# The entries of the convolution and of both attentions: order of the first two weight chunks, and of the turn of the second rows

## The reference, cut to what matters

```
u = rmsnorm(h, gain)                 # 256 x 1024
convolution:              a, gate = split(u @ w_in + b_in)      # w_in 1024 x 2048
differential attention:   q, k, v = split(h_normed @ w_qkv)     # w_qkv 1024 x 3072
dilated attention:        q = h_normed @ w_q                    # w_q 1024 x 3072
```

## Time and profile before

| what | value |
|---|---|
| three timed runs, median | 2168.71 us (2168.44 to 2171.89) |
| span of the profiled execution | 2168.2 us (no time of its own beside the span is recorded for it) |
| PE busy | 2138.8 us, 99% |
| DVE / ACT / POOL busy | 1417.4 / 1159.3 / 118.1 us |
| DMA | 371.40 MB, 171 GB/s over the span |

### The profile page before, as it was taken

One profiled execution on the slowest core, in us unless ns is written; L12 is line 12 of the kernel. 1 busy time (PEld: TensorE's weight loads), 2 busy tenths in 40 slices (PEclk: granted clock), 3 DMA queues, 4 the chain that ended last, 5 costly groups with the idle time before them and its releaser, 6 DMA issues.

```text
span 2168.2 us, 28699 instructions
## 1 busy us (share of the span) xinstructions
PE 2138.8 (99%) x11347; PEld 1789.6 (83%) x11347; DVE 1417.4 (65%) x2061; ACT 1159.3 (53%) x1711; POOL 118.1 (5%) x152
## 2 busy tenths in 40 slices
PE   9999999999999999999999999998999999999999
PEld 9878888768888878889877888787888888888887
DVE  7645765576556767657745766686656699675665
ACT  5555544536445645455555544566544565575443
POOL 0000100002000011000000200002100100000000
PEclk9999999999999999999999999999999999999999
DMA  8544655525665436555544655551655566513653
GB/s 267 184 139 163 227 189 190 180 97 181 195 194 170 152 117 195 188 190 183 185 140 159 185 189 190 183 176 59 210 190 187 181 166 188 182 61 117 200 190 115
DMA packets 190068, 371.40 MB, mean 171 GB/s; under 512 B 6993, under 2 KB 126178, under 8 KB 189808
## 3 DMA queue, kind: packets, MB, share of 16 engines
q1 hardware_dynamic: 185776, 358.70, 50.5%
q0 software_dynamic: 4160, 10.86, 2.7%
HBM read 368.48 MB, written 1.05 MB: 170 GB/s over the span
## 4 chain that ended last, share of the span: by engine, by line
PE 91%; DVE 4%; ACT 2%; POOL 1%; issue 1%; DMA 0%; SPq 0%; DVEq 0%; ACTq 0%
PE PS L663 51%; PE PS L795 14%; PE PS L797 7%; PE PS L783 5%; PE PS L833 2%; PE PS L913 1%; DVE wlo L2040 1%; PE PS L840 1%; PE PS L1115 1%; POOL wlo L2904 1%; ACT whi L1484 1%; PE PS L1393 1%; PE PS L1402 1%; PE PS L900 1%; PE PS L1216 1%
## 5 line engine op out<-in xcount | busy, mean ns | idle before, releaser
L2040 DVE TENSOR_TENSOR wlo<-raw,whi 128x1024 fp32r<-128x1024 f32 x658 | 788.7, 1225 | 195.3 <-ACT whi L1484 194.5
L1484 ACT ACTIVATE whi<-raw 128x1024 fp32r<-128x1024 f32 x680 | 700.7, 1055 | 372.3 <-PE PS L663 325.3
L663 PE MATMUL PS<-whi,U 128*128 128x512 f32 x1856 | 523.0, 397 | 7.2 <-DVE U L2078 1.9
L663 PEld LDWEIGHTS PS<-whi,U 128*128 128x128 f32 x1856 | 346.0, 189 | 90.0 <-issue 16.2
L795 PE MATMUL PS<-U,whi 128*128 128x512 f32 x1344 | 334.4, 391 | 0.0
L663 PE MATMUL PS<-wlo,U 128*128 128x512 f32 x928 | 288.2, 392 | 0.0
L795 PEld LDWEIGHTS PS<-U,whi 128*128 128x128 f32 x1344 | 246.6, 188 | 47.5
L2165 DVE TENSOR_TENSOR AR<-PS,AR 128x512 f32<-128x512 f32 x96 | 66.3, 691 | 303.5 <-ACT AR L1571 303.5
L663 PE MATMUL PS<-whi,fH 128*128 128x512 f32 x824 | 256.7, 393 | 0.9 <-DVE fL L2303 0.9
L663 PE MATMUL PS<-wlo,fH 128*128 128x512 f32 x824 | 254.4, 390 | 0.0
L663 PE MATMUL PS<-whi,fL 128*128 128x512 f32 x824 | 254.2, 390 | 0.0
(11 more groups left out here) (333 smaller groups left out, 1959.4 us busy)
## 6 DMA issues: line engine op xcount, KB each, us to landing
raw<-in_mlp_w_up SPq DMA_DIRECT2D x64, 1024.0 KB, 5.4
raw<-in_mlp_w_down SPq DMA_DIRECT2D x64, 1024.0 KB, 4.9
raw<-in_ret_w_in SPq DMA_DIRECT2D x48, 1024.0 KB, 5.2
raw<-in_m_w_up SPq DMA_DIRECT2D x32, 1024.0 KB, 5.4
raw<-in_m_w_down SPq DMA_DIRECT2D x32, 1024.0 KB, 4.9
raw<-in_kv_w SPq DMA_DIRECT2D x24, 1024.0 KB, 5.1
raw<-in_ret_w_out SPq DMA_DIRECT2D x16, 1024.0 KB, 4.7
raw<-in_gla_w_in SPq DMA_DIRECT2D x12, 1024.0 KB, 5.1
```

The lines of the kernel that those rows point to most:

```text
L663: mm = e.matmul(bank(b + nb), a, w[:, nb * 512:(nb + 1) * 512], start=(begins and n < 2), stop=(ends and n >= 4))
L1484: e.activation(split_half(whi, i, x), raw_halves(i)[x], ACT.Copy).then_inc(HI.tick((i, x)), 1)
L2040: e.tensor_tensor(split_half(wlo, i, x), raw_halves(i)[x], split_half(whi, i, x).bitcast(F32), ALU.subtract).then_inc(LO.tick((i, x)), 1)
```

## The change

All of it is in PE's program; ACT, DVE, POOL and SP keep their instructions and their order. The new `gemm_a_two` takes the first two chunks of the three stages together. Its `upper(f, k2, tt)` is the four matmuls of chunk f, half k2, rows tt with `whi` and waits for `HI` and `UL` alone; its `lower(f, k2)` is the four matmuls with `wlo` for both row groups, and signals `USED`. `turn_in` gets a list of pairs, and rows 1 are turned in two portions: pairs 0 and 1 behind the third `upper`, pairs 2 and 3 behind the fifth. The remaining two chunks go through `gemm_a` as before, with `begins=False, k_first=4`, and the convolution's filter products stay behind the third chunk. `PS` has as many matmuls and transposes written to it as before.

```diff
--- before.py
+++ after.py
@@ -746,13 +746,13 @@
...
-            def turn_in(S, tt):
+            def turn_in(S, tt, js=range(4)):
 
                 if tt == 0:
 
                     for ev in turn_free[S]:
                         e.wait_ge(*ev)
-                for j in range(4):
+                for j in js:
                     if S == RET0:
                         e.wait_ge(*s_x[tt][1])
                     else:
@@ -853,6 +853,44 @@
                 turn_in(S, 1)
                 upper(1, 1, 0)
                 upper(0, 0, 1)
+                upper(0, 1, 1)
+                lower(0, 0)
+                lower(0, 1)
+                upper(1, 0, 1)
+                upper(1, 1, 1)
+                lower(1, 0)
+                lower(1, 1)
+
+            def gemm_a_two(S):
+
+
+                i0 = first[S]
+
+                def upper(f, k2, tt):
+                    e.wait_ge(*HI[i0 + f, k2])
+                    k = 2 * f + k2
+                    e.wait_ge(*UL[(S, "in"), tt, k // 2])
+                    w = split_half(whi, i0 + f, k2)
+                    for n, a in enumerate(u_ap(k, tt)):
+                        for nb in range(2):
+                            e.matmul(bank(2 * tt + nb), a, w[:, nb * 512:(nb + 1) * 512], start=(k == 0 and n == 0), stop=False)
+
+                def lower(f, k2):
+                    e.wait_ge(*lo_cut(i0 + f, k2))
+                    w = split_half(wlo, i0 + f, k2)
+                    for tt in range(2):
+                        a_h, _ = u_ap(2 * f + k2, tt)
+                        for nb in range(2):
+                            mm = e.matmul(bank(2 * tt + nb), a_h, w[:, nb * 512:(nb + 1) * 512], start=False, stop=False)
+                    mm.then_inc(USED.tick((i0 + f, k2)), 1)
+
+                upper(0, 0, 0)
+                upper(0, 1, 0)
+                upper(1, 0, 0)
+                turn_in(S, 1, (0, 1))
+                upper(1, 1, 0)
+                upper(0, 0, 1)
+                turn_in(S, 1, (2, 3))
                 upper(0, 1, 1)
                 lower(0, 0)
                 lower(0, 1)
@@ -972,7 +1010,7 @@
                 p, c0 = PC, first[S]
 
                 def filters(c):
-                    if c != 2:
+                    if c != 0:
                         return
                     e.wait_ge(*s_conv_par[CONV_LOADS])
                     e.wait_ge(*UL[(S, "in"), 1, 3])
@@ -1028,7 +1066,8 @@
                     if tt:
                         mm.then_inc(USED.tick((i, k % 2)), 1)
 
-                gemm_a((S, 0), c0, 8, u_ap, (0, 2), fresh=fresh_u((S, "in")), entry=lambda: turn_in(S, 1), after=filters)
+                gemm_a_two(S)
+                gemm_a((S, 0), c0 + 2, 4, u_ap, (0, 2), fresh=fresh_u((S, "in")), begins=False, k_first=4, after=filters)
 
                 def beside(c):
                     if c == 1:
@@ -1219,7 +1258,8 @@
             def pe_diff(S):
                 p, c0 = PD, first[S]
                 k0, k1 = (S, 0), (S, 1)
-                gemm_a((S, 0), c0, 8, u_ap, (0, 2), fresh=fresh_u((S, "in")), entry=lambda: turn_in(S, 1))
+                gemm_a_two(S)
+                gemm_a((S, 0), c0 + 2, 4, u_ap, (0, 2), fresh=fresh_u((S, "in")), begins=False, k_first=4)
                 gemm_a((S, 1), c0 + 4, 8, u_ap, (0, 2), free=([HCP[k0 + (0,)]], [HCP[k0 + (1,)]]), entry=lambda: None)
 
                 def v_product(c):
@@ -1419,11 +1459,12 @@
                                           start=(n == 0), stop=(n == 3), skip_group_check=True)
                     mm.then_inc(VALUE.tick((S, i)), 1)
 
-                for n in range(9):
+                gemm_a_two(S)
+                gemm_a((S, 0), c0 + 2, 4, u_ap, (0, 2), fresh=fresh_u((S, "in")), begins=False, k_first=4)
+                for n in range(1, 9):
                     t = (S, "in") if n < 3 else (S, "kv")
-                    gemm_a((S, n), c0 + 4 * n, 8, u_ap, (0, 2), fresh=fresh_u(t) if n in (0, 3) else None,
-                           free=read_out(n - 1) if n else ((), ()), after=lambda c: beside(n, c),
-                           entry=(lambda: None) if n else (lambda: turn_in(S, 1)))
+                    gemm_a((S, n), c0 + 4 * n, 8, u_ap, (0, 2), fresh=fresh_u(t) if n == 3 else None,
+                           free=read_out(n - 1), after=lambda c: beside(n, c), entry=lambda: None)
 
                 for i in range(16):
                     turn(i)
```

## The result

The changed kernel takes 2172.4 us (median of 20 runs, 2169.14 to 2174.66), the kernel before 2169.47 us beside it (20 runs, 2168.27 to 2171.89): ratio 1.0014, 95% interval 1.0007 to 1.0020. The forecast was 2170.3 us and a difference of +1.6.

A forecast was written before the change was run, and what follows sets the result against it. PE's own stream was taken as the bound, busy 2138.8 of 2168.2 us. Terms +1.8 (differential attention), 0.0 (convolution) and -0.2 (dilated attention) gave +1.6 on 2168.7, so 2170.3 us, range 2167.2 to 2173.2.

The forecast's parts named there:

- Nothing is won ahead of the turn: Differential attention's entry: 0.9 us waiting for ACT replaces 0.24 + 0.68 for POOL; the turn starts at 1390.99 as before.
- Second portion 1.8 us late for ACT and DVE: Behind the turn's second portion, the last lower `U` and everything queued after it on DVE and ACT shift by about 1.8 us.
- Third chunk of the differential attention: PE would start it at 1403.08 after a new wait of 2.4 us, making the stage 1.8 us later.
- PE's own gain: At each entry, four more matmuls and four fewer transposes done by the wait for `U`: some 0.45 us gained.
- Convolution and dilated attention: Slack ahead of the third chunk hides the shift of 1.80 and 1.75 us there; results 0.0 and -0.2 us.
- The three terms: Stage effects: differential attention +1.8, convolution 0.0, dilated attention -0.2 us, summed to +1.6.
- The delay is not given back: Later waits of the differential attention shift along, so 1.8 us stands; rival, given back later: 2168.5 us, chance 0.13.
- the third chunk is bound by DVE: Differential attention: ACT and DVE cannot make up the 1.8 us; rival, not bound by DVE: 2167.2 us, chance 0.13.
- The clock in the new gap, taken as 0: Ahead of the differential attention's third chunk, 2.4 us without matmuls could cost 0 to 3.4 us; 0 taken, little confidence.
- clock falls, short: Rival: PE's clock falls once in the new gap, the shorter fall, costing 1.7 us, so 2172.0 us; chance 0.26.

The follow-up runs named there:

- diff_only: The change kept in the differential attention alone, the other two stages as in the kernel before; 2172.2 us, ratio 1.0011 to the kernel before.
- diff_back: The changed kernel with the old entry back in the differential attention alone; 2168.9 us, ratio 0.9999 to the kernel before.
- again: The changed kernel run once more as it is; 2173.6 us, ratio 1.0016 to the kernel before.
- third_first: The changed kernel, but in the differential attention ACT and DVE make the third chunk's halves ahead of exponentials and head tables; 2168.5 us, ratio 0.9994 to the kernel before.
- turn_earlier: The changed kernel with the second portion of the turn one upper sooner, behind the fourth; 2169.8 us, ratio 1.0000 to the kernel before.
- one_turn: The changed kernel with all four pairs of rows 1 turned at once behind the third upper; 2168.1 us, ratio 0.9990 to the kernel before.
- gap_transposes: The changed kernel with 19 transposes of a constant ahead of the differential attention's third chunk; 2170.9 us, ratio 1.0005 to the kernel before.

## Why the prediction was right, and which term was off

- *Nothing is won ahead of the turn*: right. The turn of rows 1 starts 0.81 us after DVE's first half of `h` in both. ACT's wait in place of POOL's is 0.78 (forecast 0.9).
- *Second portion 1.8 us late for ACT and DVE*: right, 1.80 at every step down the chain.
- *Third chunk of the differential attention*: +1.80 at its start and +1.82 in the stage's length (forecast +1.8). PE follows DVE's start by 1.28 us before and after, where I had carried 1.39; as the same distance stands on both sides, the shift was right all the same, and only the new wait came out at 2.1 us in place of 2.4. diff_only and diff_back put the loss in this stage.
- *PE's own gain*: forecast 0.45, though 4 x 0.227 less half of 1.03 is 0.39. Read from the start of the turn of rows 1, the 48 matmuls of the first two chunks would end 9.73 us later by PE's own pace (1396.28 + 8 x 0.227 - 1388.37), before 10.15: 0.42.
- *Convolution and dilated attention*: 0.0 and -0.2 forecast, 0.0 (-0.06 against again, -0.01 in diff_back against diff_only) and -0.13 measured. The three terms come to +1.7; forecast +1.6.
- *The delay is not given back*, and *the third chunk is bound by DVE*: the stage keeps the whole of it, and third_first frees the chunk by reordering ACT and DVE alone. Both rivals out.
- *The clock in the new gap, taken as 0*: this is the term that was mis-sized. It is 1.5 us in three profiles out of four. The rival "clock falls, short" had 0.26 and the forecast 0.42; the median lies at 2172.4, nearer to that rival (2172.0), and the range held it because it had been drawn to take that rival in. I called idleness of 2.4 us nearer to the wait of 1.4 than to the four one-row matmuls. For those I had also passed over the row just ahead, in the kernel before:

```profile
476.88 1.47 PE L1014 MATMUL PS<-ident,xn 128*128 128x128 f32 x8 [1.06 <-DVE xn L2409]
```

That fall too came behind a stretch in which PE stood idle, 1.06 us of it, and then did eight transposes and the four one-row matmuls; which of these it answers to is open. The Trainium skill, "TensorE: Matmul & The Clock Gate", section "Why this matters for your kernels", warns of idle gaps between bursts of matmuls, but only of gaps longer than this one. By that rule the clock would have stayed up here; in three profiles of four it fell, and the measurement decides. The changed kernel against the one before: +1.7 of delay, and +1.5 in most executions, beside a measured +2.9.
- The forecast stood on a median of three runs, 2168.7; over 20 runs the kernel before is at 2169.5. That is 0.8 us of the distance to 2172.4.

What stays open: how often the clock falls with and without the wait. It also falls in the convolution, for 3.4, 6.8 or 10.2 us: every profile shows one of the three, and the changed kernel's three profiles show all of them. The medians carry that spread; four profiles are no frequency.

## What to carry to other kernels

Before a producer's step is split to give its engine something to do in between, follow the second part down the queues that consume it: everything behind it there moves by the distance between the parts, less the time the consumer needs for the first. Here PE gained 0.4 us and two other queues did everything behind the second part 1.8 us later, which only the stage without slack showed. And a new idle stretch on TensorE may cost more than its length; fill it, or better, give the engine work that waits for nothing new, as the lower parts of rows 0 did here.

## What the runs showed of the hardware

An idle stretch of 2.1 us between dense matmuls was followed by a fall of TensorE's clock from 2.4 to 1.2 GHz in three profiles of four, 0.2 to 1.2 us after PE took up work again, and the stage was 1.5 us longer; waits of 1.1 us and less at the same place (turn_earlier, one_turn) showed none in one profile each, nor did the wait of 1.4 us later in the stage in 13 profiles. Ten float32 matmuls of a constant in that stretch went without a fall in the one profile taken, with a median 2.6 us lower. The Trainium skill, "TensorE: Matmul & The Clock Gate", section "Part 4: PE-mode transpose", says of transposes that they do not count as busy in the same way; in gap_transposes, with nineteen of them in that stretch, the granted clock stayed at 1.00 in the one profile taken. That neither bears it out nor goes against it, as one profile in four kept its clock with the stretch empty.
